# First attention: score macros of 512 columns, and row sums through a score bank

## The chip, the cores and the metric

The kernel runs on one core of one Trainium2 chip. The metric is the device time of one execution in microseconds (us). Three runs of the kernel before took 1708.31, 1708.41 and 1710.09 us; the median is 1708.41 us.

## What is computed

The reference runs a chain of blocks on 512 tokens of width 1024: a gated delta-rule layer, a feed-forward block, a forgetting-attention layer, a feed-forward block, and a last block with sparse and dense attention. The change touches only the forgetting attention, 16 heads of 64 (8 couples of heads), causal in tiles of 128 queries:

```python
for blk in range(t_len // FOX_QBLOCK):          # 4 tiles of 128 queries
    s = einsum(q[s0:e], k[:e]) * scale          # tile i sees (i + 1) * 128 keys
    s = s + log_f_cum[s0:e, None] - log_f_cum[None, :e]
    p = softmax(where(mask, s, -inf))
    outs.append(einsum(p, v[:e]))
```

So the four query tiles of a head have score rows of 128, 256, 384 and 512 columns: 1280 a head.

## The kernel before

The code places every instruction on its engine's queue by hand, and the engines meet by semaphores. The class `Pairs` (its one instance is `FIRST`) holds this attention. A couple p is two heads (r = 0, 1), which lie in partitions 0 to 63 and 64 to 127 of `Q2` and `K2`. A macro m is one piece of work for both heads of a couple. Before, a macro is one couple and one query tile, in the order 0, 3, 1, 2 of tiles: 8 x 4 = 32 macros of 128, 512, 256 and 384 columns for each head.

For each macro:

- `pe_scores`: for each head a product of Q and K (64 rows deep, so the two heads lie side by side in the array; fp32 makes two instructions of each, line L1785), then one with `sel` and `c2` that adds the forget term (L1788). The scores of head r go to a bank of PSUM; macros alternate between the banks (2, 3) and (6, 7).
- `dve_max` (L1883, VectorE): adds the mask and finds the row's extreme, which goes to `nm`.
- `exp` (L1845, ScalarE): writes `fp` and the row's sum (`rs`). Each is followed by a read of the accumulator.
- `pe_turn` (L1799, TensorE): (i + 1) transposes for each head into the banks 4 and 5 (`turned`), of which there is one set only. So the turn of macro m waits until macro m - 1 has been copied out of them.
- the copy to `fpt`: by ScalarE for the tiles 0 and 3 (L1873, 256 and 1024 elements for both heads), by VectorE for the tiles 1 and 2 (L1913, 512 and 768).
- `pe_values` (L1810): (i + 1) products for each head with `FV`, into the bank of the couple, 0 or 1 (`outs`); each is two instructions in fp32.

Once for each couple: a reciprocal of the sums (L1890, VectorE), a spread of it over rows (L1935, GpSimd), four transposes (`pe_sums`, L1820) into the output bank of the next couple, a copy of these to `fri` (L1895, VectorE), the product of output and `fri` (L1903, VectorE), and the split of the result into `hT_hi` (L1863, ScalarE) and `hT_lo` (L1940, GpSimd), which the output projection FO reads.

TensorE's order in iteration m is: scores of m, a hook, `pe_sums`, turn of m - 1, values of m - 2. ScalarE's is: the two exps of m, its copy of m - 1, `act_high`. VectorE's is: the two maxima of m, its copy of m - 1, reciprocal, spread, final. The scores of macros 0 and 1 are made ahead of the last slot of the Q projection; ScalarE and VectorE take that slot out of PSUM (L1956, L1964), and ScalarE also makes a weight split (`act_split`, L145), before they begin with `FIRST.act(2)` and `FIRST.dve(2)`. At the end, two pieces of FO's first weight slot (L338, L343, L346) are put as hooks between the last macros, and FO goes on after the last values. Behind FO come the second feed-forward block and the last block, all of them led by TensorE.

Of the kernel before, what the change touches and what calls it, by code (L numbers as in the profile page):

```python
# [75 lines left out]
def program(nc, x_in, wpack, wba, wf, gains, convw, vecs, consts, masks, out):  # L76
    ctx = ExitStack()
    with ctx:
# [1682 lines left out]
        class Pairs:  # L1761
# [5 lines left out]
            ORDER = (0, 3, 1, 2)  # L1767

            def __init__(self, banks, turned, outs):
                self.macros = [(p, i) for p in range(FP) for i in self.ORDER]  # L1770
                self.banks, self.turned, self.outs = banks, turned, outs
                self.nm, self.rs, self.ri = stat(4), stat(2 * len(self.macros)), stat(2 * len(self.macros))
                self.n = len(self.macros)

            def score(self, m, r):
                return PS[:, self.banks[m % 2][r], 0:(self.macros[m][1] + 1) * P]

            def pe_scores(self, m):
                t = nc.tensor
                p, i = self.macros[m]  # L1780
                if m >= 2:
                    t.wait_ge(sem("fx_exp"), 2 * (m - 2) + 2)
                for r in range(2):
                    x = slice(64 * r, 64 * r + 64)
                    t.matmul(self.score(m, r), Q2[x, p, i * P:(i + 1) * P], K2[x, p, 0:(i + 1) * P], start=True, stop=False)  # L1785
                for r in range(2):
                    x = slice(64 * r, 64 * r + 64)
                    t.matmul(self.score(m, r), sel[x, 2 * p + r:2 * p + r + 1].to_broadcast([64, P]), c2[x, 0:(i + 1) * P],  # L1788
                             start=False, stop=True).then_inc(sem("fx_score"), 1)

            def pe_turn(self, m):
                t = nc.tensor
                i = self.macros[m][1]
# [6 lines left out]
                last.then_inc(sem("fx_turned"), 1)  # L1800

            def pe_values(self, m):
                t = nc.tensor
                p, i = self.macros[m]
                t.wait_ge(sem("fx_pt"), m + 1)
                if m % 4 == 0 and p >= 1:
                    t.wait_ge(sem("fx_inv"), p)
                for j in range(i + 1):
                    for r in range(2):
                        last = t.matmul(PS[64 * r:64 * r + 64, self.outs[p % 2], i * P:(i + 1) * P], FV[:, j, (2 * p + r) * FD:(2 * p + r + 1) * FD],  # L1810
                                        fpt[m % 2][:, r, j * P:(j + 1) * P], start=(j == 0), stop=(j == i))
                last.then_inc(sem("fx_pv"), 1)

            def pe_sums(self, p):
                t = nc.tensor
                t.wait_ge(sem("fx_rows"), p + 1)
                if p:
                    t.wait_ge(sem("fx_final"), p)
                for i in range(TT):
                    last = t.transpose(PS[:, self.outs[(p + 1) % 2], i * P:(i + 1) * P], frs[:, i, :, :].rearrange("p r d -> p (r d)"), ident)  # L1820
                last.then_inc(sem("fx_sums"), 1)

            def pe(self, begun, hooks):
# [12 lines left out]
            def exp(self, m):  # L1836
                a = nc.scalar
                w = (self.macros[m][1] + 1) * P
                for r in range(2):
                    n = 2 * m + r  # L1840
                    a.wait_ge(sem("fx_max"), n + 1)
                    if m >= 2:
                        a.wait_ge(sem("fx_turned"), m - 1)
                    c = 8 * self.macros[m][0] + 2 * self.macros[m][1] + r
                    a.activation(fp[m % 2][:, r, 0:w], self.score(m, r), ACT.Exp, bias=self.nm[:, n % 4:n % 4 + 1], scale=-1.0,  # L1845
                                 accum_out=self.rs[:, c:c + 1]).then_inc(sem("fx_exp"), 1)

            def copy_ready(self, eng, m):
                eng.wait_ge(sem("fx_turned"), m + 1)
                if m >= 2:  # L1850
                    eng.wait_ge(sem("fx_pv"), m - 1)

            def copy_views(self, m):
                w = (self.macros[m][1] + 1) * P
                return fpt[m % 2][:, :, 0:w], PS[:, self.turned[0]:self.turned[0] + 2, 0:w]

            def by_vector(self, m):
                return self.macros[m][1] in (1, 2)
# [6 lines left out]
            def act(self, begun):  # L1865
                a = nc.scalar
                for m in range(self.n + 1):
                    if begun <= m < self.n:
                        self.exp(m)
                    if m >= 1 and not self.by_vector(m - 1):  # L1870
                        self.copy_ready(a, m - 1)
                        o, i = self.copy_views(m - 1)
                        a.activation(o, i, ACT.Copy).then_inc(sem("fx_pt"), 1)  # L1873
                    if m >= 7 and m % 4 == 3:
                        self.act_high(m // 4 - 1)
                self.act_high(FP - 1)

            def dve_max(self, m):
                v = nc.vector
                for r in range(2):  # L1880
                    n = 2 * m + r
                    v.wait_ge(sem("fx_score"), n + 1)
                    v.tensor_tensor_reduce(out=self.score(m, r), in0=self.score(m, r), in1=mask_row(0, self.macros[m][1]),  # L1883
                                           scale=-1.0, scalar=-MAX_NEG, op0=ALU.add, op1=ALU.min,
                                           accum_out=self.nm[:, n % 4:n % 4 + 1]).then_inc(sem("fx_max"), 1)

            def dve_inverse(self, p):
                v = nc.vector
                v.wait_ge(sem("fx_exp"), 8 * p + 8)
                v.reciprocal(self.ri[:, 8 * p:8 * p + 8], self.rs[:, 8 * p:8 * p + 8]).then_inc(sem("fx_ri"), 1)  # L1890

            def dve_spread(self, p):
                v = nc.vector
                v.wait_ge(sem("fx_sums"), p + 1)
                v.tensor_copy(fri[:, :], PS[:, self.outs[(p + 1) % 2], :]).then_inc(sem("fx_inv"), 1)  # L1895

            def dve_final(self, p):
                v = nc.vector
                v.wait_ge(sem("fx_inv"), p + 1)
                v.wait_ge(sem("fx_pv"), 4 * p + 4)  # L1900
# [4 lines left out]
            def dve(self, begun):  # L1905
                v = nc.vector
                for m in range(self.n + 1):
                    if begun <= m < self.n:
                        self.dve_max(m)
                    if m >= 1 and self.by_vector(m - 1):  # L1910
                        self.copy_ready(v, m - 1)
                        o, i = self.copy_views(m - 1)
                        v.tensor_copy(o, i).then_inc(sem("fx_pt"), 1)  # L1913
                    if m % 4 == 0 and m >= 4:
                        self.dve_inverse(m // 4 - 1)
                    if m % 4 == 1 and m > 4:
                        self.dve_spread(m // 4 - 1)
                    if m % 4 == 2 and m > 4:
                        self.dve_final(m // 4 - 1)
                self.dve_spread(FP - 1)  # L1920
                self.dve_final(FP - 1)
# [45 lines left out]
        def pe_fox_scores():  # L1967
# [3 lines left out]
            nc.tensor.wait_ge(sem("sel"), 4)  # L1971
# [43 lines left out]
        def act_foxproj():  # L2015
# [23 lines left out]
            a.wait_ge(sem("c_zero"), 1)  # L2039
# [10 lines left out]
        def dve_foxproj():  # L2050
            v = nc.vector
            dve_heads("fk", K2, 1.0)
            v.memset(c2[:, :].bitcast(F32), 0.0).then_inc(sem("c_zero"), 1)
# [29 lines left out]
        def pe_fox():  # L2083
# [13 lines left out]
            def first_tile(tt, n):  # L2097
                t.wait_ge(sem("fx_exp"), n)
# [3 lines left out]
            FIRST.pe(2, {2: last_heads, n: lambda: first_tile(1, 2 * n - 2), n + 1: lambda: first_tile(3, 2 * n)})  # L2102
            slot(1, [1], False)
            t.wait_ge(sem("fx_pt"), n)
# [929 lines left out]
```

## Time and profile before

| | us |
|---|---|
| median of three runs | 1708.41 |
| the profiled execution | 1710.62 |
| its span, first to last instruction | 1708.8 |
| TensorE busy in the span | 1681.0 |
| VectorE, ScalarE, GpSimd busy | 587.9, 653.0, 688.8 |
| the attention: first score to last value | 858.6 to 952.0 |
| mean granted clock of TensorE | 0.994 |

Times are counted from the start of the span. The timeline gives the start of a run of like instructions and how long they lasted; the ends of matmuls are modelled and reach over the start of the next, so what a group occupies on TensorE is best read from its start to the next group's start. The granted clock is 1.00 at 2.4 GHz and 0.50 at 1.2 GHz.

### The profile page before, as it was taken

What the parts mean: (1) busy time and instruction counts of PE and PEld (TensorE: products, weight loads), DVE (VectorE), ACT (ScalarE), POOL (GpSimd) and SP (SyncE); (2) the same over time, 40 slices, a digit from 0 to 9 for tenths busy, and PEclk for the clock granted to TensorE, in tenths of its full rate; (3) what the DMA queues carried; (4) which work ended last, traced back from release to release, by engine and by line L of the source; (5) the groups of instructions that cost most, each with busy time, mean ns of one, the idle gap of its engine ahead of it and who ended that gap; (6) DMA issues with size and microseconds to landing.
All of it is one profiled execution on the core that took longest, in us unless ns stands there. A gap on an engine that the chain in (4) does not pass through costs nothing.

```text
span 1708.8 us, 23543 instructions
## 1 busy us (share of the span) xinstructions
PE 1681.0 (98%) x9382; PEld 1405.3 (82%) x9382; DVE 587.9 (34%) x1176; ACT 653.0 (38%) x988; POOL 688.8 (40%) x538
## 2 busy tenths in 40 slices
PE   6999999999999999999999999999999999999999
PEld 6787889898888888887866898888888887887887
DVE  3359325440100001521146240100011545788661
ACT  4653534442222222522356342222222535554651
POOL 3533233434444455544322434444455433554002
PEclk9999899999999999999999999999999999999999
DMA  5212110422222322232220122222322232222001
GB/s 197 74 54 95 51 50 26 160 75 99 98 98 98 110 99 98 72 126 99 75 75 2 52 73 99 98 98 98 127 99 98 92 106 99 75 78 95 26 2 49
DMA packets 23427, 145.00 MB, mean 85 GB/s; under 512 B 3504, under 2 KB 4272, under 8 KB 7344
## 3 DMA queue, kind: packets, MB, share of 16 engines
q1 hardware_dynamic: 23344, 143.83, 24.0%
q8 instruction: 59, 0.97, 0.2%
q14 instruction: 24, 0.20, 0.0%
HBM read 141.72 MB, written 2.10 MB: 84 GB/s over the span
## 4 chain that ended last, share of the span: by engine, by line
PE 68%; issue 14%; POOL 10%; DVE 5%; ACT 2%; DMA 1%; SPq 0%; POOLq 0%; ACTq 0%; DVEq 0%
POOL wlo L2804 10%; PE PS L452 5%; PE PS L453 5%; PE PS L454 5%; PE PS L485 4%; PE PS L343 4%; PE PS L346 4%; PE PS L338 4%; PE PS L486 4%; PE PS L487 4%; PE PS L961 2%; PE PS L466 2%; PE PS L467 2%; PE PS L468 2%; PE PS L1642 2%
## 5 line engine op out<-in xcount | busy, mean ns | idle before, releaser
L2804 POOL TENSOR_TENSOR wlo<-wraw,whi 128x512 fp32r<-128x512 f32 (+1 forms) x476 | 628.3, 1352 | 907.2 <-ACT whi L145 907.2
L145 ACT ACTIVATE whi<-wraw 128x2048 fp32r<-128x2048 f32 (+1 forms) x119 | 225.7, 1896 | 239.9 <-PE PS L346 183.6
L452 PE MATMUL PS<-hT_hi,whi 128*128 128x512 f32 x704 | 274.0, 389 | 0.0
L453 PE MATMUL PS<-hT_lo,whi 128*128 128x512 f32 x704 | 273.9, 389 | 0.0
L454 PE MATMUL PS<-hT_hi,wlo 128*128 128x512 f32 x704 | 273.9, 389 | 0.0
L1544 DVE TENSOR_TENSOR act_sb<-sil,PS 128x512 f32 x44 | 30.3, 688 | 428.5 <-ACT sil L1519 428.5
L1519 ACT ACTIVATE sil<-PS 128x512 f32<-128x512 f32 x44 | 26.4, 599 | 355.3 <-PE PS L454 335.4
L452 PEld LDWEIGHTS PS<-hT_hi,whi 128*128 128x128 f32 x704 | 132.2, 188 | 28.0 <-issue 0.6
L454 PEld LDWEIGHTS PS<-hT_hi,wlo 128*128 128x128 f32 x704 | 132.2, 188 | 27.5
L453 PEld LDWEIGHTS PS<-hT_lo,whi 128*128 128x128 f32 x704 | 132.2, 188 | 27.2
L485 PE MATMUL PS<-whi,hT_hi 128*128 128x512 f32 (+2 forms) x288 | 112.3, 390 | 0.1
L487 PE MATMUL PS<-whi,hT_lo 128*128 128x512 f32 (+2 forms) x288 | 110.4, 384 | 0.0
L486 PE MATMUL PS<-wlo,hT_hi 128*128 128x512 f32 (+2 forms) x288 | 110.4, 383 | 0.0
L343 PE MATMUL PS<-wlo,ahi 128*128 128x512 f32 x352 | 109.0, 390 | 0.6 <-POOL wlo L2804 0.6
L338 PE MATMUL PS<-whi,ahi 128*128 128x512 f32 x352 | 108.8, 390 | 0.2
L346 PE MATMUL PS<-whi,alo 128*128 128x512 f32 x352 | 108.4, 389 | 0.0
L1549 DVE TENSOR_TENSOR alo<-act_sb,ahi 128x1024 fp32r<-128x1024 f32 x22 | 29.3, 1340 | 177.2 <-ACT ahi L1508 177.2
L343 PEld LDWEIGHTS PS<-wlo,ahi 128*128 128x128 f32 x352 | 66.1, 188 | 15.1 <-POOL wlo L2804 1.4
L338 PEld LDWEIGHTS PS<-whi,ahi 128*128 128x128 f32 x352 | 65.8, 188 | 14.4 <-POOL wlo L2804 1.1
L601 DVE SCALAR_TENSOR_TENSOR cva<-PS,small,cva 128x511 f32<-128x511 f32 (+2 forms) x72 | 53.8, 748 | 68.7 <-ACT cva L592 66.8
L346 PEld LDWEIGHTS PS<-whi,alo 128*128 128x128 f32 x352 | 66.1, 188 | 13.7
L466 PE MATMUL PS<-hT_hi,whi 128*128 128x256 f32 x224 | 64.7, 289 | 2.3 <-DVE hT_lo L289 2.3
(410 smaller groups left out, 3057.8 us busy)
## 6 DMA issues: line engine op xcount, KB each, us to landing
wraw<-wpack SPq DMA_DIRECT2D x125, 1024.0 KB, 4.9
gain<-gains SPq DMA_DIRECT2D x10, 512.0 KB, 6.6
x_sb<-x SPq DMA_DIRECT2D x8, 512.0 KB, 6.4
out<-x_sb SPq DMA_DIRECT2D x3, 512.0 KB, 2.6
csb<-consts SPq DMA_DIRECT2D x1, 704.0 KB, 13.7
out<-x_sb SPq DMA_DIRECT2D x2, 256.0 KB, 2.0
vh<-vecs SPq DMA_DIRECT2D x1, 96.0 KB, 6.4
small<-vecs SPq DMA_DIRECT2D x1, 80.0 KB, 12.1
```

The lines of the kernel that those rows point to most:

```text
L145: act.activation((whi[q % 2] if static is not None else hi_of_slot(n))[:, w], wraw[q % 2][:, w], ACT.Copy).then_inc(w_hi, 1)
L338: nc.tensor.matmul(PS[:, 2 * t + half, :], lhi(kk, t), whi[q][:, kk * D + half * 512:][:, 0:512], start=a, stop=False)
L343: nc.tensor.matmul(PS[:, 2 * t + half, :], lhi(kk, t), wlo[q][:, kk * D + half * 512:][:, 0:512], start=False, stop=False)
L346: last = nc.tensor.matmul(PS[:, 2 * t + half, :], llo(kk, t), whi[q][:, kk * D + half * 512:][:, 0:512], start=False, stop=b)
L452: nc.tensor.matmul(o, whi[q][w], hT_hi[:, k, :], start=(k == 0), stop=False)
L453: nc.tensor.matmul(o, whi[q][w], hT_lo[:, k, :], start=False, stop=False)
L454: last = nc.tensor.matmul(o, wlo[q][w], hT_hi[:, k, :], start=False, stop=(k == KT - 1))
L466: nc.tensor.matmul(o, hi_of_slot(n)[w], hT_hi[:, k, ts], start=(k == 0), stop=False)
L485: nc.tensor.matmul(o, hi[:, k0 + kk, ts], hi_of_slot(n)[w], start=(first and kk == 0), stop=False)
L486: nc.tensor.matmul(o, hi[:, k0 + kk, ts], lo_of_slot(n)[w], start=False, stop=False)
L487: last = nc.tensor.matmul(o, lo[:, k0 + kk, ts], hi_of_slot(n)[w], start=False, stop=(final and kk == nk - 1))
L2804: p.tensor_tensor(lo[:, a:b], wraw[q][:, a:b], hi[:, a:b].bitcast(F32), ALU.subtract).then_inc(w_lo, 1)
```

## The change

A macro now always fills a bank of 512 columns for each head: tile 3 of a couple; tiles 0 and 2 of a couple, at the columns 0 and 128; or tile 1 of two neighbouring couples, at the columns 0 and 256. Two couples make five macros, in the order (0, 2), (3), (1, 1'), (0', 2'), (3'), so there are 20 in place of 32. The columns, the transposes and the products are the same in number. The maxima and the exps stay one for each tile and head; an exp waits for all the maxima of its head in the macro. Every turn has 8 transposes, with a signal for each head. The copies go by a list: of five macros, the first is ScalarE's (VectorE's in the first five), the second is half each, the third VectorE's, the fourth ScalarE's, the fifth half each.

The sums of a couple that ended in macro e are turned into the first score bank of macro e + 1, once that macro's exps are done, in iteration e + 2 and behind its turn; the scores of macro e + 3, which use this bank again, wait for the spread. The sums of the last couple go to bank 4. Several waits of FO follow suit, and two start signals (`c_zero`, `sel`) become one.

```diff
-            ORDER = (0, 3, 1, 2)
             def __init__(self, banks, turned, outs):
-                self.macros = [(p, i) for p in range(FP) for i in self.ORDER]
+                self.macros, self.copies = [], []
+                for p in range(0, FP, 2):
+                    self.macros += [[(p, 0, 0), (p, 2, P)], [(p, 3, 0)], [(p, 1, 0), (p + 1, 1, 2 * P)], [(p + 1, 0, 0), (p + 1, 2, P)],
+                                    [(p + 1, 3, 0)]]
+                    self.copies += ["a" if p else "v", "av", "v", "a", "av"]
...
+            def sums_bank(self, p):
+                m = self.ends[p] + 1
+                return PS[:, self.banks[m % 2][0] if m < self.n else self.turned[0], :]
...
             def pe_scores(self, m):
-                    t.wait_ge(sem("fx_exp"), 2 * (m - 2) + 2)
...
+                    t.wait_ge(sem("fx_exp"), self.u0[m - 1])
+                    for p in self.ended(m - 3):
+                        t.wait_ge(sem("fx_spread"), p + 1)
...
             def pe_turn(self, m):
-                    t.wait_ge(sem("fx_pt"), m)
+                    self.copied(m - 1)
                 for r in range(2):
-                    t.wait_ge(sem("fx_exp"), 2 * m + r + 1)
-                    for j in range(i + 1):
+                    t.wait_ge(sem("fx_exp"), self.u0[m] + (r + 1) * len(self.macros[m]))
+                    for j in range(TT):
...
             def pe(self, begun, hooks):
-                    if m % 4 == 1 and m > 4:
-                        self.pe_sums(m // 4 - 1)
                     if 0 <= m - 1 < self.n:
                         self.pe_turn(m - 1)
+                    for p in self.ended(m - 2):
+                        if m <= self.n:
+                            self.pe_sums(p)
                     if 0 <= m - 2 < self.n:
                         self.pe_values(m - 2)
+                self.pe_sums(FP - 1)
...
             def act(self, begun):
+                for m in range(self.n + 4):
                     if begun <= m < self.n:
                         self.exp(m)
+                    if 0 <= m - 1 < self.n:
+                        self.act_copy(m - 1)
+                    for p in self.ended(m - 4):
+                        self.act_high(p)
...
             def dve(self, begun):
+                for m in range(self.n + 3):
                     if begun <= m < self.n:
                         self.dve_max(m)
...
+                    if 0 <= m - 1 < self.n:
+                        self.dve_copy(m - 1)
+                    for p in self.ended(m - 1):
+                        if m < self.n:
+                            self.dve_inverse(p)
+                    for p in self.ended(m - 2):
+                        self.dve_spread(p)
+                    for p in self.ended(m - 3):
+                        self.dve_final(p)
```

## Rows read from the trace of the kernel before

**Rows 1.** The page, its first part: busy time, share of span, instructions.
```profile
PE 1681.0 (98%) x9382; PEld 1405.3 (82%) x9382; DVE 587.9 (34%) x1176; ACT 653.0 (38%) x988; POOL 688.8 (40%) x538
```

**Rows 2.** Waits, 868 to 954: waiter, releaser, us in total, times, longest.
```profile
PE PS L1799 <- ACT fpt L1873: 3.5, 8, 2.0
```

**Rows 3.** Timeline of TensorE, 896.5 to 907.5: start, us, line, form, count.
```profile
896.14 1.13 PE L1785 MATMUL PS<-K,Q 64*128 64x512 f32 x4
...
897.46 0.66 PE L1820 MATMUL PS<-csb,frs 128*128 128x128 f32 x4
897.95 0.38 PE L1799 MATMUL PS<-csb,fp 128*128 128x128 f32 x2
...
900.10 1.09 PE L1799 MATMUL PS<-csb,fp 128*128 128x128 f32 x8 [0.22 <-ACT fpt L1873]
901.12 0.44 PE L1810 MATMUL PS<-fpt,FV 128*64 128x128 f32 x4
...
903.10 1.09 PE L1810 MATMUL PS<-fpt,FV 128*64 128x128 f32 x16
904.12 0.49 PE L1785 MATMUL PS<-K,Q 64*128 64x128 f32 x4
...
904.61 0.88 PE L1799 MATMUL PS<-csb,fp 128*128 128x128 f32 x6
...
906.00 1.13 PE L1785 MATMUL PS<-K,Q 64*128 64x512 f32 x4
```

**Rows 4.** Windows: span, busy us of PE, PEld, DVE, ACT, POOL; PEclk, DMA, GB/s.
```profile
897.00:907.00 10.00, 9.78 (x92) 6.55 (x88) 6.73 (x21) 6.22 (x19) 1.99 (x3) 1.00 0.01 2
```

**Rows 5.** Timeline of TensorE, 857.5 to 882: the start of the attention.
```profile
858.61 0.49 PE L1785 MATMUL PS<-K,Q 64*128 64x128 f32 x4
...
859.00 1.08 PE L1785 MATMUL PS<-K,Q 64*128 64x512 f32 x4
...
865.86 0.38 PE L1799 MATMUL PS<-csb,fp 128*128 128x128 f32 x2
866.17 0.70 PE L1785 MATMUL PS<-K,Q 64*128 64x256 f32 x4
866.52 0.47 PE L1788 MATMUL PS<-c,sel 64*128 64x256 f32 x2
868.98 1.06 PE L1799 MATMUL PS<-csb,fp 128*128 128x128 f32 x8 [2.00 <-ACT fpt L1873]
```

**Rows 6.** Chain of waits, 866 to 956: start, us, what.
```profile
897.54 0.69 DVE PS L1883
...
898.33 0.02 ACT fp L1845
```

**Rows 7.** Groups by shape, 877.7 to 937.5: six couples; busy us, mean ns.
```profile
L1845 ACT ACTIVATE fp<-PS,small 128x512 f32<-128x512 f32 x12 | 8.1, 682 | 13.7 <-DVE small L1883 13.7
...
L1845 ACT ACTIVATE fp<-PS,small 128x384 f32<-128x384 f32 x12 | 6.9, 577 | 5.4 <-DVE small L1883 5.4
...
L1873 ACT ACTIVATE fpt<-PS 128x1024 f32<-128x1024 f32 x6 | 6.1, 1021 | 0.0
L1913 DVE COPY fpt<-PS 128x768 f32<-128x768 f32 x6 | 5.7, 958 | 1.2 <-PE PS L1799 1.2
...
L1845 ACT ACTIVATE fp<-PS,small 128x128 f32<-128x128 f32 x12 | 4.3, 363 | 0.4
...
L1863 ACT ACTIVATE hT_hi<-fo_t 128x512 fp32r<-128x512 f32 x6 | 3.8, 626 | 0.0
```

**Rows 8.** Timeline of ScalarE, 857.5 to 885: what it did meanwhile.
```profile
866.55 1.90 ACT L145 ACTIVATE whi<-wraw 128x2048 fp32r<-128x2048 f32 x1
```

**Rows 9.** Windows of 1 us at the start of the attention.
```profile
871.00:872.00 1.00, 1.00 (x6) 0.25 (x2) 0.00 (x0) 0.11 (x1) 1.00 (x2) 0.50 0.00 0
...
873.00:874.00 1.00, 1.00 (x11) 0.94 (x12) 0.86 (x3) 1.00 (x4) 0.48 (x1) 0.50 0.00 0
```

**Rows 10.** Timeline of GpSimd, 830 to 1010: the last split.
```profile
953.60 1.30 POOL L1940 TENSOR_TENSOR hT_lo<-fo_t,hT_hi 128x512 fp32r<-128x512 f32 x1 [3.30 <-ACT hT_hi L1863]
```

**Rows 11.** Timeline of TensorE, 925.5 to 978: behind the last values.
```profile
951.99 0.74 PE L338 MATMUL PS<-whi,hT_hi 128*128 128x512 f32 x2
```

More of the change, by code:

```diff
@@ new lines, in __init__ @@
+                for p in range(0, FP, 2):
+                    self.macros += [[(p, 0, 0), (p, 2, P)], [(p, 3, 0)], [(p, 1, 0), (p + 1, 1, 2 * P)], [(p + 1, 0, 0), (p + 1, 2, P)],
+                                    [(p + 1, 3, 0)]]
+                    self.copies += ["a" if p else "v", "av", "v", "a", "av"]
+                self.n = len(self.macros)
+                self.banks, self.turned, self.outs = banks, turned, outs
+                self.u0 = [2 * sum(len(x) for x in self.macros[:m]) for m in range(self.n + 1)]
@@ new lines, in __init__, with pairs, ended @@
+                self.by = {e: [sum(e in c for c in self.copies[:m]) for m in range(self.n + 1)] for e in "av"}
+                self.begins = {p: min(m for m in range(self.n) if p in self.pairs(m)) for p in range(FP)}
+                self.ends = {p: max(m for m in range(self.n) if p in self.pairs(m)) for p in range(FP)}
+                self.nm, self.rs, self.ri = stat(8), stat(8 * FP), stat(8 * FP)
+            def pairs(self, m):
+                return [p for p, _, _ in self.macros[m]]
+            def ended(self, m):
+                return [p for p in range(FP) if self.ends[p] == m]
@@ L1778, in pe_scores, with units, score @@
+            def units(self, m):
+                n = len(self.macros[m])
+                return [(self.u0[m] + r * n + k, r, k) for r in range(2) for k in range(n)]
+            def score(self, m, r, k):
+                _, i, c = self.macros[m][k]
+                return PS[:, self.banks[m % 2][r], c:c + (i + 1) * P]
+            def sums_bank(self, p):
+                m = self.ends[p] + 1
+                return PS[:, self.banks[m % 2][0] if m < self.n else self.turned[0], :]
             def pe_scores(self, m):
@@ new lines, in pe_scores @@
+                    for p in self.ended(m - 3):
+                        t.wait_ge(sem("fx_spread"), p + 1)
+                for k, (p, i, _) in enumerate(self.macros[m]):
+                    for r in range(2):
+                        x = slice(64 * r, 64 * r + 64)
+                        t.matmul(self.score(m, r, k), Q2[x, p, i * P:(i + 1) * P], K2[x, p, 0:(i + 1) * P], start=True, stop=False)
+                    for r in range(2):
+                        x = slice(64 * r, 64 * r + 64)
+                        t.matmul(self.score(m, r, k), sel[x, 2 * p + r:2 * p + r + 1].to_broadcast([64, P]), c2[x, 0:(i + 1) * P],
+                                 start=False, stop=True).then_inc(sem("fx_score"), 1)
@@ L1799, in pe_turn @@
                         last = t.transpose(PS[:, self.turned[r], j * P:(j + 1) * P], fp[m % 2][:, r, j * P:(j + 1) * P], ident)
[L1800 to L1812, printed above, removed]
+                    last.then_inc(sem("fx_turned"), 1)
@@ L1816, in pe_sums, with pe_values @@
                 t.wait_ge(sem("fx_rows"), p + 1)
-                if p:
-                    t.wait_ge(sem("fx_final"), p)
                 for i in range(TT):
-                    last = t.transpose(PS[:, self.outs[(p + 1) % 2], i * P:(i + 1) * P], frs[:, i, :, :].rearrange("p r d -> p (r d)"), ident)
+                    last = t.transpose(self.sums_bank(p)[:, i * P:(i + 1) * P], frs[:, i, :, :].rearrange("p r d -> p (r d)"), ident)
                 last.then_inc(sem("fx_sums"), 1)
+            def pe_values(self, m):
+                t = nc.tensor
+                self.copied(m)
+                for p in self.pairs(m):
+                    if p >= 2 and self.begins[p] == m:
+                        t.wait_ge(sem("fx_final"), p - 1)
+                for p, i, c in self.macros[m]:
+                    for j in range(i + 1):
+                        for r in range(2):
+                            last = t.matmul(PS[64 * r:64 * r + 64, self.outs[p % 2], i * P:(i + 1) * P], FV[:, j, (2 * p + r) * FD:(2 * p + r + 1) * FD],
+                                            fpt[m % 2][:, r, c + j * P:c + (j + 1) * P], start=(j == 0), stop=(j == i))
+                last.then_inc(sem("fx_pv"), 1)
             def pe(self, begun, hooks):
@@ L1837, in exp @@
                 a = nc.scalar
[L1838 to L1841, printed above, removed]
+                for n, r, k in self.units(m):
+                    p, i, c = self.macros[m][k]
+                    a.wait_ge(sem("fx_max"), self.u0[m] + (r + 1) * len(self.macros[m]))
                     if m >= 2:
[L1843 to L1846, printed above, removed]
@@ L1850, in copy_ready, with act_copy @@
                 if m >= 2:
                     eng.wait_ge(sem("fx_pv"), m - 1)
[L1853 to L1858, printed above, removed]
+            def act_copy(self, m):
+                a = nc.scalar
+                if self.copies[m] == "a":
+                    self.copy_ready(a, m, 1)
+                    a.activation(fpt[m % 2][:, :, :], PS[:, self.turned[0]:self.turned[0] + 2, :], ACT.Copy).then_inc(sem("fx_pt_a"), 1)
+                if self.copies[m] == "av":
+                    self.copy_ready(a, m, 0)
+                    a.activation(fpt[m % 2][:, 0, :], PS[:, self.turned[0], :], ACT.Copy).then_inc(sem("fx_pt_a"), 1)
@@ L1860, in act_high, with dve_copy @@
+            def dve_copy(self, m):
+                v = nc.vector
+                if self.copies[m] == "v":
+                    self.copy_ready(v, m, 1)
+                    v.tensor_copy(fpt[m % 2][:, :, :], PS[:, self.turned[0]:self.turned[0] + 2, :]).then_inc(sem("fx_pt_v"), 1)
+                if self.copies[m] == "av":
+                    self.copy_ready(v, m, 1)
+                    v.tensor_copy(fpt[m % 2][:, 1, :], PS[:, self.turned[1], :]).then_inc(sem("fx_pt_v"), 1)
             def act_high(self, p):
@@ L1905, in dve @@
             def dve(self, begun):
-                v = nc.vector
-                for m in range(self.n + 1):
+                for m in range(self.n + 3):
                     if begun <= m < self.n:
                         self.dve_max(m)
[L1910 to L1921, printed above, removed]
+                    for p in self.ended(m - 1):
+                        if m == self.n:
+                            self.dve_inverse(p)
+                    if 0 <= m - 1 < self.n:
+                        self.dve_copy(m - 1)
+                    for p in self.ended(m - 1):
+                        if m < self.n:
+                            self.dve_inverse(p)
+                    for p in self.ended(m - 2):
+                        self.dve_spread(p)
+                    for p in self.ended(m - 3):
+                        self.dve_final(p)
             def pool(self):
```

67 lines of the change are left out of this document (27 added, 40 removed).

## The prediction, made before the changed kernel ran

> **What bounds the kernel now.** I read the page first: TensorE is busy for 1681.0 of 1708.8 us [rows 1], so a change pays by TensorE time that it takes away, or by TensorE idle time that it closes. Then the list of waits over the attention: TensorE idled there for 3.5 us in 8 places, always in front of a turn that waits for ScalarE's copy out of the turned banks [rows 2]. The longest was 2.0 us; the other seven share 1.5, some 0.22 each. Then the timeline of TensorE for one couple, which repeats to a few hundredths: 896.14 to 906.00, so 9.86 us a couple, of which 0.22 idle in front of the turn of tile 3 [rows 3]. The other engines are far from full: in 10 us VectorE has 6.73 and ScalarE 6.22 us of work [rows 4]. So the stage is bound by TensorE's own work, and by a chain (scores, maximum, exp, copy, next turn) that comes 0.22 us late once for each couple.
>
> **TensorE's groups.** The reader is to see here is that a group costs less for each instruction when it is long. All by start to next start: a turn of 8 costs 900.10 to 901.12 = 1.02 us, a turn of 2 costs 0.31 (897.95 on, the same in row 865.86 to 866.17 of [rows 5]). That makes 0.118 for a transpose and 0.07 for the group. Values of 16 instructions cost 903.10 to 904.12 = 1.02. Scores of 512 columns cost 896.14 to 897.46 = 1.32, of 128 columns 904.12 to 904.61 = 0.49, and of 256 columns 866.17 to 866.52 + 0.47 = 0.82 [rows 3, 5]: 0.277 for 128 columns and 0.21 for the group. A set of sums costs 897.46 to 897.95 = 0.49 [rows 3].
>
> **New work for two couples.** The number of columns, transposes and products is the same; only the groups are fewer. Five turns: 5 x 1.02 = 5.10. Five values: 5.10. Two sums: 0.98. Scores: two macros of one tile at 1.32 = 2.64, and three of two tiles. A two-tile group is not in the steady trace. Its lower bound is a single group of 512 columns, 1.32. Its upper bound is two groups in a row at their full price: 0.49 + 1.04 (384 columns, between its neighbours) = 1.53 for tiles 0 and 2, and 2 x 0.82 = 1.64 for the two tiles 1. Nearest is the start, where the 128 columns of macro 0 are directly followed by macro 1: 858.61 to 859.00 = 0.39, so 0.10 less than 0.49 [rows 5]. I take 0.39 + 1.04 = 1.43, three times 4.29. The sum is 5.10 + 5.10 + 0.98 + 2.64 + 4.29 = 18.11 us, against 2 x 9.86 = 19.72 with the idle time and 19.28 without it.
>
> **Do the others keep up?** The turned banks are single, so the turn of m waits for the copy of m - 1, and on ScalarE that copy stands behind the exps of m. Take S as the start of the scores of m. Maxima start 0.08 us after the scores end and an exp starts 0.79 us after the maximum (897.54 to 898.33) [rows 6]. One tile: exps from S + 2.19, two of 0.68, to 3.55; a full copy of 1.02 [rows 7] to S + 4.57; with 0.05 us for the signal (an estimate) TensorE may turn at S + 4.62. TensorE's own way there is scores, turn, values and next scores: 1.32 + 1.02 + 1.02 + 1.32 or more = 4.68 or more. On time. Two tiles: two maxima per head come first, so exps start at S + 1.43 + 0.08 + 0.90 = 2.41; they take 2 x (0.577 + 0.363) = 1.88, to 4.29; then half a copy. 512 columns out of PSUM on ScalarE are not there in this stage; the same width from SBUF took 0.626, the 1024 took 1.02 and I take 0.60: 4.89, with the signal 4.94 [rows 7]. TensorE's own way is 1.43 + 2.04 + 1.32 = 4.79 behind (0, 2), and 4.90 behind (1, 1'). So a stall of 0.15 and one of 0.04 in five macros: 0.2. Two of the five iterations also hold a set of sums, which gives 0.49 us of slack. Where VectorE copies all of it, the copy (1024 elements; its 768 took 0.96 [rows 7], so near 1.3 for 1024) comes behind four maxima that take no longer than their exps, 1.88: by S + 1.51 + 1.88 + 1.3 = 4.69 of 4.79. Fine. Two couples: 18.11 + 0.2 = 18.3 against 19.72, a gain of 1.4; four times 5.7 us.
>
> The Trainium skill gives another price for that half copy. "ScalarE: Activation LUTs", Rules for kernel authors, budgets about 0.3 us for an instruction and 0.83 ns for an element, thus some 0.72 us for 512 as an estimate. The row above for the same width has 0.626. With the page's price the two stalls would be 0.27 and 0.16 and the sum 1 us worse; the row decides.
>
> **The new wait for the bank of the sums.** Scores of e + 3 wait for the spread. What is queued behind that wait on TensorE is everything: turn, values. Sums end at 1.32 + 1.02 + 0.49 = S + 2.83 in their iteration, VectorE is through with its two maxima by S + 2.76 (1.40, and no more than the two exps take, 1.36) and its list has no copy there. The spread moves 512 columns, so it takes less than the 0.96 us of 768 [rows 7], and ends before S + 2.83 + 0.96 = 3.79; TensorE wants the bank at S + 3.85. Cost 0, but it is close. The two start signals that merge, the additional signal of each turn and the waits (41 in place of 44 for two couples) cost nothing I can see: bound 0 to 0.02 us a macro, 0.4 in all, in the range.
>
> **The start.** Before, the turn of macro 0 runs at 865.86 and the next scores to 866.99; then TensorE idles for 2.0 us until 868.98 [rows 5], because the copy of macro 0 stands on ScalarE behind the weight split of 1.90 us [rows 8]. Behind that gap the granted clock was 0.50, the 1.2 GHz level, in three windows of 1 us, 871 to 874 [rows 9]: 1.5 us of work lost, 1.6 with the edges. Now VectorE copies macro 0. From the end of the turn the copy takes about 0.1 + 1.3 us, and TensorE has two-tile scores of 1.43 in between: no idle. Gain 2.0 less the 0.22 that I have already counted = 1.8. And without the gap I expect the clock to stay: in the steady couples, with the same mixture of work and 0.22 of idle, it was 1.00 [rows 4]. Gain 1.6. The larger scores ahead of the last Q slot are a shift of work (about 1 us earlier on the path) and are in the 18.11.
>
> **The end.** FO's pieces stay between the last macros. The last sums now come behind the last values, and spread, product and the two splits after them. Before, the last split ended at 954.9 [rows 10], and FO went on at 951.99 [rows 11] with six pieces of near 2.9 us that don't need it. That cover of over 10 us stays. Cost 0. All that follows is led by TensorE and shifts as a whole.
>
> **The sum.** 5.7 + 1.8 + 1.6 = 9.1 us. Laid out once more from the first turn (865.86) to 951.99, 86.1 us before and 76.2 + 1.0 now, it is 8.9. I take 9.0: a span of 1699.8 against 1708.8. The profiled run took 1710.62 and the median is 1708.41; I take the gain off the median: 1699.4.
>
> **Rivals.**
>
> *The copy is late in every macro.* ScalarE's chain of 4.94 us has no slack. If its parts are 0.15 to 0.3 us longer in place (more signals, a wait of an exp for two maxima), each of 18 macros stalls by that: 2.7 to 5.4 us, so 1702 to 1705. For it: the margins above are 0.06 to 0.1. Against: a stall delays the next scores as well, so two macros share it. 15%. The Trainium skill has the same worry: "TensorEngine Tiling (Array Packing)", PSUM Bottleneck, says that work packed on TensorE does not speed up the way out of PSUM, which may then become the limit, and advises to use ScalarE and VectorE both; the lists of copies do so.
>
> *The start stays slow.* The copy on VectorE is late, or the clock falls without a gap: 1.6 to 3.4 us back, 1701 to 1703. The clock alone gives 1701.0. For it: the margin of the copy is 0.03 us, and the start has turns, values and 64-row scores only, no long projection matmuls. Against: the steady couples are the same mixture and stood at a clock of 1.00 [rows 4]. 17%.
>
> *Slower.* The chain from the scores to the copied macro sets the rhythm. Two macros can't be shorter than this chain L plus turn and values, L + 2.04. With L = 4.94 that is 6.98 for two, as TensorE needs. Each us on L costs half a us for each macro, 9 us over 18. From L = 5.9 the gain is gone, from 6.3 the kernel is slower by over 0.2%: 1712 and more. It would need the exps and maxima of two tiles in one bank to get in each other's way for over 1 us in 3. VectorE works on head 1's bank while ScalarE reads head 0's, as before. 5%.
>
> *It does not do what it says.* Groups cost by instruction and not by group: then the two-tile scores cost 1.5 to 1.6, 1.3 us in all, and the turns and values keep their measured prices. That is a part of my range and no case by itself. Something later that takes most of the gain (a weight transfer that TensorE now reaches too soon) would give 1705 to 1709: 5%.
>
> **Chances.** Forecast 58%, with 1697.5 (scores at the lower bound, no stalls) to 1701; the start 17%; late copies 15%; lost later 5%; slower 5%. The range 1696.5 to 1705 takes in the first three but for their edges. A measurement can tell about 0.2%, 3.4 us, so faster is below 1705.0. Faster 0.88, same 0.06, slower 0.06.
>
> **What would show it.** Turns of 8 at 1.02 us; two-tile scores at 1.43 from start to start; 18.3 us for five macros; the stall in front of the turns of macros 5k and 5k + 2 at 0.15 us or less; nothing waiting for the spread; no gap behind 866.8 and a clock of 1.00 between 870 and 875. Wrong would be: idle time in front of most turns, or ScalarE busy for nearly all of an iteration.

## The result, and the profile after

The changed kernel took 1696.39 us (median of 4 runs, 1695.70 to 1697.95), the kernel before beside it 1708.36: a ratio of 0.9934, with a 95% interval of 0.9921 to 0.9947. A later comparison of the same two, on another occasion, gave 1697.69 against 1706.98, 0.9944 (0.9931 to 0.9958). The ratios here and below are not the quotients of the two medians; the two can differ by up to 0.001. The forecast was 1699.4 in a range of 1696.5 to 1705.0.

The profiled execution of the changed kernel took 1696.14 us, its span 1694.3. The page's first part:

```profile
PE 1669.6 (99%) x9382; PEld 1401.0 (83%) x9382; DVE 585.4 (35%) x1173; ACT 652.6 (39%) x987; POOL 689.0 (41%) x538
```

TensorE has the same 9382 instructions as in [rows 1] and is busy for 11.4 us less. The waits of TensorE inside the attention, from the list of waits (860 to 945), are down to one of 0.2 us, while [rows 2] had eight with 3.5 us:

```profile
PE PS L1826 <- DVE fpt L1893: 0.2, 1, 0.2
```

The list misses stalls of 0.1 to 0.2 us, because the modelled end of a matmul reaches over them; only a comparison of starts shows these.

The timeline of TensorE, first the start of the attention (compare [rows 5]), then five steady macros (compare [rows 3]). Columns: start, length, line, form, count. L1809 and L1812 are the scores, L1826 the turns, L1833 the sums, L1845 the values.

```profile
862.72 1.03 PE L1826 MATMUL PS<-csb,fp 128*128 128x128 f32 x8
863.69 0.70 PE L1809 MATMUL PS<-K,Q 64*128 64x256 f32 x4
...
865.28 1.06 PE L1826 MATMUL PS<-csb,fp 128*128 128x128 f32 x8 [0.22 <-DVE fpt L1893]
...
870.70 1.13 PE L1809 MATMUL PS<-K,Q 64*128 64x512 f32 x4
...
871.98 1.09 PE L1826 MATMUL PS<-csb,fp 128*128 128x128 f32 x8
872.91 0.60 PE L1833 MATMUL PS<-csb,frs 128*128 128x128 f32 x4
873.44 1.09 PE L1845 MATMUL PS<-fpt,FV 128*64 128x128 f32 x16
874.47 0.49 PE L1809 MATMUL PS<-K,Q 64*128 64x128 f32 x4
...
874.86 0.86 PE L1809 MATMUL PS<-K,Q 64*128 64x384 f32 x4
...
875.83 1.09 PE L1826 MATMUL PS<-csb,fp 128*128 128x128 f32 x8
876.85 1.09 PE L1845 MATMUL PS<-fpt,FV 128*64 128x128 f32 x16
877.87 1.13 PE L1809 MATMUL PS<-K,Q 64*128 64x512 f32 x4
...
879.31 1.09 PE L1826 MATMUL PS<-csb,fp 128*128 128x128 f32 x8
...
881.79 0.70 PE L1809 MATMUL PS<-K,Q 64*128 64x256 f32 x4
...
882.45 0.60 PE L1809 MATMUL PS<-K,Q 64*128 64x256 f32 x4
...
883.09 1.09 PE L1826 MATMUL PS<-csb,fp 128*128 128x128 f32 x8
...
892.39 0.49 PE L1809 MATMUL PS<-K,Q 64*128 64x128 f32 x4
```

Two couples take 874.47 to 892.39 = 17.92 us, against 19.72 before. The gap behind the first turn is gone but for 0.2 to 0.3 us. What is left of it is not a late copy. VectorE's timeline has the copy of macro 0:

```profile
863.79 1.23 DVE L1893 COPY fpt<-PS 128x1024 f32<-128x1024 f32 x1 [0.18 <-PE PS L1826]
```

It ended at 865.02, when the two-tile scores were just through (863.69 and their 1.30 us, as at 881.79, make 864.99). The turn began at 865.28, 0.26 us after the copy's end.

The windows of 10 us show a full clock where [rows 9] had 0.50:

```profile
860.00:870.00 10.00, 9.78 (x83) 7.71 (x83) 5.35 (x18) 5.48 (x15) 4.61 (x4) 1.00 0.10 43
870.00:880.00 10.00, 9.92 (x97) 6.89 (x93) 7.26 (x23) 6.37 (x22) 1.59 (x3) 1.00 0.61 212
```

**Where the time went.** The attention is best taken from its first score to FO's first piece behind the last values. The first scores of the changed kernel start at 854.67, FO goes on at 937.53: 82.86 us. Before these were 858.61 and 951.99 [rows 5, 11]: 93.38. So the change took 10.5 us off the attention. Behind it nothing moved: 1694.3 - 937.53 = 756.8 us against 1708.8 - 951.99 = 756.8. Ahead of it the two traces differ by 3.9 us, in code that is the same in both. This is not the change: in nine traces of eight kernels the attention began at 858.6 and 854.6 (both with the old attention), 854.7 and 855.9 (both the changed kernel), 855.2, 855.3, 856.7, 857.4 and 858.5 (other experiments), and the lower clock stood in other windows between 10 and 230 us each time. The kernel before alone took 1704.90 us at a mean clock of 0.997 and 1712.38 at 0.993 in 20 executions of one comparison. So up to 4 us of a single difference of spans is this scatter, and the 12.0 us of the first comparison are 10.5 of change and some 1.5 of it; the second comparison gave 9.3. Each kernel but the changed one has one trace only, and the trace of the kernel before is of an execution with a low mean clock (0.994). Whether the clock falls inside its attention in every execution isn't known, and 1.5 us of the 10.5 hang on that.

### The profile page after: what moved, and what is told of

The parts are those of the page before. It is cut to its first block, busy times and chain, and to the rows that moved or that the text cites. A ratio compares the mean times of both kernels' runs of the same rounds, so it can differ in the third digit from the quotient of the medians.

```text
span 1694.3 us, 23544 instructions
## 1 busy us (share of the span) xinstructions
PE 1669.6 (99%) x9382; PEld 1401.0 (83%) x9382; DVE 585.4 (35%) x1173; ACT 652.6 (39%) x987; POOL 689.0 (41%) x538
## 4 chain that ended last, share of the span: by engine, by line
PE 68%; issue 13%; POOL 10%; DVE 5%; ACT 2%; DMA 1%; SPq 0%; POOLq 0%; ACTq 0%; DVEq 0%
POOL wlo L2839 10%; PE PS L452 5%; PE PS L454 5%; PE PS L453 5%; PE PS L485 4%; PE PS L343 4%; PE PS L346 4%; PE PS L338 4%; PE PS L487 4%; PE PS L486 4%; PE PS L961 2%; PE PS L466 2%; PE PS L467 2%; PE PS L468 2%; PE PS L1642 2%
## 6 DMA issues: line engine op xcount, KB each, us to landing
small<-vecs SPq DMA_DIRECT2D x1, 80.0 KB, 11.4
```

## The experiments

In all of them the length of the attention is from the first score to FO's first piece behind the last values (and the last sums, where they come last).

### The start alone

```diff
             def by_vector(self, m):
-                return self.macros[m][1] in (1, 2)
+                return self.macros[m][1] in (1, 2) or m == 0
```

> The kernel before, with one edit: VectorE in place of ScalarE copies macro 0 (256 elements) out of the turned banks. It does the start of the change alone. Theory: the 2.0 us gap behind the first turn goes, but the copy of macro 1 now waits on ScalarE for the same weight split (to 868.35 in the trace before), then for two exps (0.92) and its own 1.02, so it is done near 870.3, while TensorE wants the next turn near 869.4. A new gap of 0.9 to 1.0 us stands one turn later; 1.0 to 1.1 us are gained. If the clock falls only behind a gap of about 2 us, it stays at 1.00 and another 1.6 us come back: 2.6 in all, near 1705.8 us. Rival: the clock falls behind the shorter gap too, or without a gap (the start has no long projection matmuls): gain 1.0 us, and windows at 0.50 near 871 to 874.

Measured: 1705.50 us against 1707.97, ratio 0.9991 (0.9981 to 1.0000). The interval says little more than a gain of 0 to 3 us. The trace says more: the attention takes 854.64 to 945.40 = 90.76 us, 2.6 less than before. TensorE's timeline:

```profile
861.89 0.38 PE L1799 MATMUL PS<-csb,fp 128*128 128x128 f32 x2
...
863.37 1.06 PE L1799 MATMUL PS<-csb,fp 128*128 128x128 f32 x8 [0.35 <-DVE fpt L1913]
...
866.37 0.66 PE L1799 MATMUL PS<-csb,fp 128*128 128x128 f32 x4 [0.54 <-ACT fpt L1873]
```

Instead of one gap of 2.0 us there are two of 0.35 and 0.54. The second stands behind the copy of macro 1, as expected, but it was forecast at 0.9 to 1.0 and alone; the sum came out right. The clock was 1.00 in every window of the start:

```profile
864.00:866.00 2.00, 1.82 (x14) 0.89 (x12) 0.14 (x1) 2.00 (x6) 1.43 (x2) 1.00 0.00 0
866.00:868.00 2.00, 1.63 (x22) 1.30 (x22) 1.69 (x5) 1.54 (x5) 2.00 (x2) 1.00 0.00 0
```

So 1.0 us came from the gaps (by starts 2.05 before and 1.04 here) and the other 1.6 from the clock. The kernel before bears this out. Its TensorE ran the same eight groups, from the turn of 8 to the next scores of 512 columns, behind the gap and in every couple. Behind the gap they ended with this row of its timeline:

```profile
876.42 1.13 PE L1785 MATMUL PS<-K,Q 64*128 64x512 f32 x4
```

From 868.98 [rows 5] to 876.42 they took 7.44 us, and from 900.10 to 906.00 [rows 3] 5.90: 1.5 us lost.

### The start undone

```diff
-                    self.copies += ["a" if p else "v", "av", "v", "a", "av"]
+                    self.copies += ["a", "av", "v", "a", "av"]
```

> The changed kernel with ScalarE's copy of macro 0 put back. Theory: this copy (1.02 us) stands behind the weight split, so the second turn comes about 1.0 us later than in the changed kernel (a gap of 1.3 in place of 0.3); its copy of macro 1 stays hidden. Price 1.0 us, 1697.4, if the clock stays at 1.00; 2.6 us, 1699.0, if it falls behind this gap. Rival (the start was worth what the prediction said, 3.4 us, in the changed kernel as well): 1699.8.

Measured: 1698.81 us, ratio 0.9952 (0.9935 to 0.9969) against before. The attention takes 855.23 to 939.26 = 84.03 us, 1.2 more than in the changed kernel. The gap in TensorE's timeline:

```profile
866.99 1.06 PE L1826 MATMUL PS<-csb,fp 128*128 128x128 f32 x8 [1.39 <-issue]
```

And windows of 2 us from 866 on, with the granted clock third from the end:

```profile
866.00:868.00 2.00, 1.01 (x10) 0.87 (x10) 1.28 (x8) 2.00 (x7) 2.00 (x2) 1.00 0.00 0
868.00:870.00 2.00, 2.00 (x29) 1.67 (x28) 0.69 (x1) 1.10 (x5) 2.00 (x3) 1.00 0.04 8
```

"issue" is where the profile names no releaser; in the code the turn waits for ScalarE's copy there. A gap of 1.4 us in place of 0.2 cost 1.2 us and no clock, so here the choice of engine is worth 1.2 us. The time alone doesn't decide this: the interval reaches from 1696.9 to 1703 us and takes in the rival's 1699.8. The start of before had lost some 3.5 us in all (2.0 idle, 1.5 by the clock). About 2.1 of them came back by the longer macros themselves, without another engine for the copy. They give TensorE 1.2 us more to do while the weight split runs, the copy behind the split is 0.6 us longer (1.01 for 0.38), so the gap is 1.4 and not 2.0, and the clock stayed at 1.00 in this trace.

### The way of the sums alone

The macros of before in the new code:

```diff
-                for p in range(0, FP, 2):
-                    self.macros += [[(p, 0, 0), (p, 2, P)], [(p, 3, 0)], [(p, 1, 0), (p + 1, 1, 2 * P)], [(p + 1, 0, 0), (p + 1, 2, P)],
-                                    [(p + 1, 3, 0)]]
-                    self.copies += ["a" if p else "v", "av", "v", "a", "av"]
+                for p in range(FP):
+                    self.macros += [[(p, i, 0)] for i in (0, 3, 1, 2)]
+                    self.copies += ["a", "a", "v", "v"]
...
-                    for j in range(TT):
+                    for j in range(self.width(m) // P):
```

(and the copies cut to that width)

> The new code with the 32 old macros of one couple and one tile, in the old order and with the old copies: only the way of the sums through a score bank, behind the turn, is new. Theory: TensorE's groups are those of before, so nothing is gained; and the new wait costs. Sums are done 2.1 us after the start of tile 3's scores, VectorE is busy with tile 3's maxima to 2.7, the spread takes 0.69 to 3.45, but TensorE wants the bank for the next scores at 2.93: 0.5 us late, of which 0.3 take the place of the old stall of 0.3 in front of the turn of tile 3. So 0.2 us a couple slower, 1 to 2 us in all: near 1710. Rival (the way of the sums brings a part of the gain, since the output bank of the next couple is no longer held): 1 to 4 us faster than before.

Measured: 1710.03 us, ratio 1.0016 (1.0007 to 1.0026): slower. The attention takes 856.68 to 953.12 = 96.44 us, 3.1 more than before. From the list of TensorE's waits (840 to 960):

```profile
PE PS L1811 <- DVE fri L1932: 3.6, 7, 0.5
```

And one of the seven places in TensorE's timeline:

```profile
939.76 0.67 PE L1811 MATMUL PS<-K,Q 64*128 64x256 f32 x3 [0.52 <-DVE fri L1932]
```

The scores of tile 1 wait 0.52 us for the spread, once a couple. The sign was as expected, the size was not: the couple takes 10.32 us (875.68 to 937.57 for six) in place of 9.86, so 0.46 more and not 0.2. The old stall did vanish into the new wait, as forecast: the scores at 939.76 have 0.76 us to the turn at 940.52, which is their own price. What the forecast lacked is a stall one macro on, too short for the list of waits. TensorE's timeline, then ScalarE's:

```profile
910.97 0.92 PE L1811 MATMUL PS<-K,Q 64*128 64x384 f32 x4
...
912.16 0.66 PE L1828 MATMUL PS<-csb,fp 128*128 128x128 f32 x4
```

```profile
911.08 1.02 ACT L1886 ACTIVATE fpt<-PS 128x1024 f32<-128x1024 f32 x1
```

The same in the kernel before:

```profile
901.50 0.92 PE L1785 MATMUL PS<-K,Q 64*128 64x384 f32 x4
...
902.51 0.66 PE L1799 MATMUL PS<-csb,fp 128*128 128x128 f32 x4
```

These scores take 1.19 us to the turn here and 1.01 there. The exps of tile 1 are as late as its scores, ScalarE's copy of tile 3 stands behind them and ends at 912.10, and the turn follows 0.06 us later. So the new way of the sums is no gain by itself; it is what the sharing of a macro by two couples needs (the output bank of the second couple is in use when the first ends), and of the kernels here it was free only in those with long macros around it.

This kernel also has the start of before, and its windows of 1 us show the clock again, behind a gap of 1.95 us:

```profile
866.00:867.00 1.00, 0.00 (x0) 0.03 (x1) 0.00 (x0) 1.00 (x3) 0.40 (x1) 1.00 0.00 0
...
868.00:869.00 1.00, 1.00 (x8) 0.50 (x8) 0.00 (x0) 0.71 (x1) 1.00 (x1) 0.50 0.00 0
...
870.00:871.00 1.00, 1.00 (x6) 0.30 (x3) 0.20 (x1) 0.00 (x0) 1.00 (x2) 0.50 0.06 16
```

### A longer chain on ScalarE

```diff
-                    self.copies += ["a" if p else "v", "av", "v", "a", "av"]
+                    self.copies += ["a" if p else "v", "a", "a", "a", "a"]
```

> The changed kernel with all copies but the first by ScalarE, whole (1.02 us each). It makes the chain from scores to copied macro longer by 0.4 us behind two-tile macros, on purpose. Theory (two macros in a row share one delay, since a stall also delays the next scores): stalls of 0.55 to 0.6 us in front of the turns of two of five macros, 1.1 for two couples in place of 0.2: 3.7 us slower than the changed kernel, 1700.1. Rival (each macro pays): three stalls, 1.7 for two couples, 6 us slower, 1702.4. Rival (ScalarE becomes the bound): its work for two couples is 8.2 of exps, 5.1 of copies and 1.3 of splits, 14.6 us, so it should not.

Measured: 1700.72 us, ratio 0.9956 (0.9941 to 0.9971). The attention takes 858.49 to 944.68 = 86.19 us, 3.3 more than in the changed kernel; "shared" gave 3.7, "each pays" 6. TensorE's timeline over five macros:

```profile
889.99 0.49 PE L1809 MATMUL PS<-K,Q 64*128 64x128 f32 x4
...
891.84 1.09 PE L1826 MATMUL PS<-csb,fp 128*128 128x128 f32 x8 [0.43 <-ACT fpt L1884]
...
895.25 1.09 PE L1826 MATMUL PS<-csb,fp 128*128 128x128 f32 x8
...
899.09 1.09 PE L1826 MATMUL PS<-csb,fp 128*128 128x128 f32 x8
...
903.00 1.09 PE L1826 MATMUL PS<-csb,fp 128*128 128x128 f32 x8 [0.50 <-ACT fpt L1884]
...
908.83 0.49 PE L1809 MATMUL PS<-K,Q 64*128 64x128 f32 x4
```

There are two stalls of 0.4 to 0.5 us (0.5 to 0.6 by starts) in five macros, and the turn after a stalled one is late by less than 0.1 us: the next scores were put off as well. That is the rhythm by pairs that the rival "slower" was built on, and it also says why that rival was far. Two of five copies are longer by 0.4 us, a third moved from VectorE to ScalarE, and two couples take 18.84 us (889.99 to 908.83) in place of 17.92, so 0.9 more.

### More copies on VectorE

```diff
-                    self.copies += ["a" if p else "v", "av", "v", "a", "av"]
+                    self.copies += ["a" if p else "v", "v", "v", "a", "v"]
```

> The changed kernel with VectorE in place of both engines for the halved copies: of five macros, VectorE copies three whole (1.23 us each) and ScalarE two. Theory (the stalls of 0.12 and 0.15 us behind two-tile macros come from ScalarE's half copy): both go, 17.65 in place of 17.92 us for two couples, 1.0 us less from first score to last value, 81.9; in the time 0 to 1 us. Rival (VectorE becomes late with the next maxima, since the copy, a reciprocal and a final stand in one iteration): 17.9 to 18.2 for two couples, up to 1 us more.

Measured: 1696.28 us, ratio 0.9940 (0.9927 to 0.9954), beside 1697.69 and 0.9944 of the changed kernel on the same chip: not to be told apart by the time. The attention takes 855.30 to 937.48 = 82.18 us against 82.90 of the changed kernel in that comparison, 0.7 less. TensorE's timeline:

```profile
875.09 0.49 PE L1809 MATMUL PS<-K,Q 64*128 64x128 f32 x4
...
878.50 1.13 PE L1809 MATMUL PS<-K,Q 64*128 64x512 f32 x4
...
879.78 1.09 PE L1826 MATMUL PS<-csb,fp 128*128 128x128 f32 x8
...
892.79 0.49 PE L1809 MATMUL PS<-K,Q 64*128 64x128 f32 x4
```

The scores at 878.50 take 1.28 us to the turn, where the changed kernel needs 877.87 to 879.31 = 1.44. Two couples take 17.70 us in place of 17.92. So 17.70 is TensorE's work and 0.22 was the stall behind the half copies, where I had forecast 0.2. ScalarE's timeline of the changed kernel has the half copy:

```profile
878.65 0.61 ACT L1887 ACTIVATE fpt<-PS 128x512 f32<-128x512 f32 x1
```

It ended at 879.26, and the turn began at 879.31. In the kernel with more copies on it, VectorE's timeline prints no wait from 883.67 to 889.9, and VectorE is still in time.

### The changed kernel again

> The changed kernel itself, to be compared with the two below on the same chip, and for a second trace. Both theories: near 1696.4 us; from the first score to FO's first piece behind the last values 82.9 us as in its first trace, whatever the start of the attention is (it stood at 854.7 there and at 858.6 in the trace before, and lay between these in four more traces of both sorts).

Measured: 1697.69 us, ratio 0.9944 (0.9931 to 0.9958). The attention takes 855.89 to 938.79 = 82.90 us, 0.04 from its first trace, though it starts 1.2 us later.

### Half of the change

```diff
-                for p in range(0, FP, 2):
-                    self.macros += [[(p, 0, 0), (p, 2, P)], [(p, 3, 0)], [(p, 1, 0), (p + 1, 1, 2 * P)], [(p + 1, 0, 0), (p + 1, 2, P)],
-                                    [(p + 1, 3, 0)]]
-                    self.copies += ["a" if p else "v", "av", "v", "a", "av"]
+                for p in range(FP):
+                    self.macros += [[(p, 0, 0), (p, 2, P)], [(p, 3, 0)], [(p, 1, 0)]]
+                    self.copies += ["a" if p else "v", "av", "v"]
```

(and the turn and the copies cut to the width, as above)

> Half of the change: tiles 0 and 2 share a macro, tile 3 and tile 1 have one each, three macros for a couple, 24 in all (copies: ScalarE, halves, VectorE). Theory: TensorE's work for two couples grows by the groups of tile 1 (two turns at 0.59 for one at 1.02, two values likewise, two scores at 0.70 for one at 1.30) to about 18.1 us, and the chain is late by about 0.5 us a couple: the full copy of (0, 2) stands on ScalarE behind tile 3's exps until 4.57 us after tile 3's scores start, and TensorE's own way is 1.29 + 1.02 + 0.44 + 0.59 + 0.70 = 4.04. So 19.1 for two couples, 4.5 us slower than the changed kernel, near 1701. Rival (only the number of groups counts): 18.1, 1 us slower. Rival (only long macros without short ones keep the score bank of the sums free: scores wait for the spread as with one-tile macros): the wait shows in front of tile 1's scores, 0.4 to 0.5 us a couple.

Measured: 1703.57 us, ratio 0.9978 (0.9969 to 0.9987). The attention takes 857.39 to 945.67 = 88.28 us: 5.4 more than the changed kernel, 5.1 less than before. A couple takes 9.61 us, so 19.22 for two, where 19.1 was expected, but the stalls are not only where I had put them. TensorE's timeline at tile 1's scores:

```profile
886.29 0.67 PE L1811 MATMUL PS<-K,Q 64*128 64x256 f32 x3 [0.29 <-ACT fp L1874]
...
887.18 1.10 PE L1828 MATMUL PS<-csb,fp 128*128 128x128 f32 x8
```

ScalarE's timeline, the last exp of tiles 0 and 2 ahead of 886.29:

```profile
883.24 0.59 ACT L1874 ACTIVATE fp<-PS,small 128x384 f32<-128x384 f32 x1
```

VectorE's timeline, the spread:

```profile
885.45 0.69 DVE L1932 COPY fri<-PS 128x512 f32<-128x512 f32 x1
```

The 0.29 us stand in front of tile 1's scores. The profile names ScalarE, but the exps that these scores wait for (of tiles 0 and 2) were done at 883.8. The other wait in the code is the spread, and VectorE ended it at 886.14; the scores started 0.15 us later, much as the 0.14 in the kernel with the old macros (its spread ended at 939.62, its scores started at 939.76). So this is the second rival: the score bank is still held by the sums. The rest, 0.1 to 0.2 us, is the copy in front of tile 3's turn: ScalarE ended it at 887.13, and the turn began at 887.18. The half of the change that lets two couples share a macro is therefore worth more than the 1 us of its groups: it also takes away the only short iteration, in which both waits came due.

## Why the prediction was right, and where it was not

- **What bounds.** Right: TensorE's own work. The maximum, exp and copy chain cost 0.22 us for two couples, the forecast 0.2 (shown by the kernel with more copies on VectorE). That it came so near is partly luck: the chain from the scores at 874.47 ended after 4.79 us and not 4.89, and TensorE's own way to the turn took 4.68 and not 4.79, so two errors of 0.1 cancelled.
- **TensorE's work for two couples.** Forecast 18.11, measured 17.70: this term was mis-sized, by 1.6 us over the attention, and it is nearly all of the difference between 9.0 and 10.5. Three parts. Two-tile scores took 874.47 to 875.83 = 1.36 and 881.79 to 883.09 = 1.30, where I took 1.43: 0.27 in all. The error was in the single prices: for 384 columns I went between neighbours (1.04), where the trace of before has 901.50 to 902.51 = 1.01, and behind another tile it is 0.97; for 256 columns I took the modelled end of the last record (0.82), where the start of the next group says 0.66 for the first and 0.64 for the second of a pair. Single tiles of 512 took 1.28 and not 1.32: 0.08. And a set of sums directly behind a turn took with it 871.98 to 873.44 = 1.46, not 1.51: 0.1. In these rows a group was about 0.1 us shorter when the same kind of matmul followed (scores of 128 columns 0.39 against 0.49, a turn of 8 0.93 with sums behind it against 1.02 with values), and I had counted too few of the changes of kind that disappear.
- **The stall before.** I read 0.22 a couple from the idle time that the profile prints. A single group of 256 columns costs about 0.66 + 0.10 = 0.76 by the starts (0.76 also at 939.76 in the kernel with the sums alone), and in the trace of before these scores started at 899.07, 1.03 ahead of the turn at 900.10 [rows 3], so it was 0.27. Small, in the same direction.
- **The start.** Right in the main: the gap went from 2.05 to 0.29 us by starts, less the 0.27 already counted 1.5, where 1.8 was forecast; for the clock 1.6 was forecast, 1.5 is what before had lost, and it stayed at 1.00. The reason (no gap of 2 us, no lower clock) is borne out by all nine starts: gaps of 1.95 and 2.0 us were followed by 3 us at 1.2 GHz in both traces that had them, gaps of 0.2 to 0.8 us (seven, in six traces) and the one of 1.4 us by none. The start alone is the cleanest of them, since only the gap was split there. What between 1.4 and 2.0 decides is open. The 0.29 us that stayed had no term in the prediction. The copy took 1.23 us and not 1.3 and was done with the scores, as forecast; but the turn came 0.26 us after it, and the sum had nothing there.
- **The wait for the sums' bank.** Right that it costs nothing here, and that it is close: the spread ends at 881.57, with 0.14 us of signal 881.71, and the scores start at 881.79. In two kernels with a shorter macro around it, TensorE stood for it 0.3 to 0.5 us a couple.
- **The end.** Right: FO followed the last sums at once, and 756.8 us remained behind it in both.
- **ScalarE's half copy.** 0.60 us was forecast; the trace has 0.61 (878.65 on). The estimate of 0.72 by the Trainium skill ("ScalarE: Activation LUTs", Rules for kernel authors) was too high for this form; the two stalls were 0.22 together and not 0.43.
- **The rivals.** Late copies in every macro did not come; two macros share one delay, as said against it and as shown with the longer chain. "Slower" would have needed a chain of 6.3 us; adding 0.4 us to it on two macros of five cost 3.3 us in all. The start did not stay slow.
- **The range.** It ended at 1696.5, and the first comparison has 1696.39, the second 1697.69. So the time lies at its lower edge, the first median 0.1 us outside; 0.9934 of the 1708.41 from which the forecast was made is 1697.1, inside. It had no term for the part ahead of the attention, which moves single spans by up to 4 us.

In the sum: 5.7 forecast for the steady macros, 4 x 1.80 = 7.2 measured; 3.4 forecast for the start, 1.5 of gap and 1.5 of clock measured, 3.0. That makes 10.2, against 10.5 from first score to FO; 0.3 us I can't place.

## What to carry to other kernels

When TensorE bounds a stage and its work is many small groups, count the groups and the changes from one kind of matmul to another, not only the instructions; and take the price of a group from its start to the start of the next, never from a modelled end. A bank that is borrowed for a moment is free only if the iteration around it is longer than the chain that gives it back; packing that removes the short iterations pays twice. A late group also makes the work of the next engine late, so look one macro on for a second, smaller stall. A gap on TensorE may cost more than its idle time (here 2.0 us idle and 1.5 by the clock), so look at the granted clock in the few us behind it before pricing its removal.

## What the runs showed of the hardware that I had not expected

- A gap of 1.95 to 2.0 us on TensorE was followed, about 1 to 2 us after work began again, by 3 us at 1.2 GHz (two kernels, one trace each); a gap of 1.4 us in the same place was not (one trace).
- Matmuls on 64 rows, whose two heads lie side by side: a group of 128 columns took 0.39 us when scores followed and 0.49 when a turn followed.
- In the steady macros a wait for ScalarE's copy was over about 0.05 us after the end of its record (879.26 to 879.31), one for VectorE's spread after 0.14 to 0.15. At the second turn of the attention it took 0.20 to 0.29 us in all nine traces, whichever engine had copied (VectorE 865.02 to 865.28 in the changed kernel, ScalarE 868.73 to 868.98 in the kernel before). The code gives no reason, and no run looks for one.
- The part ahead of the attention differs by up to 4 us from trace to trace, in code that is the same. Where the lower clock falls differs too, but it isn't shown to be all of it: the second trace of the changed kernel had no window below 1.00 before 190 us, where the first had some from 15 on, and began its attention 1.2 us later.
